# Up group 1 of the second feed-forward as pairs of seven quarter products, with the weight sums made by accumulating transfers

## The reference

```python
def _sqrelu_mlp(h, w1, w2):
    return jnp.square(jax.nn.relu(h @ w1)) @ w2

    h2 = _modulate(_rmsnorm(x, norm2_g), sh2, sc2)
    x = x + g2 * _sqrelu_mlp(h2, w_ff1, w_ff2)
```

## Time and profile before

| | |
|---|---|
| three runs | 1659.97, 1660.47, 1660.49 us |
| median | 1660.47 us |
| profiled execution | 1660.74 us, of which the profile's span is 1659.0 us |
| TensorE busy in the span | 98% |
| VectorE, ScalarE, GpSimd busy | 67%, 46%, 9% |
| second feed-forward | from 1300.7 us of the span to its end |

### The profile page before, as it was taken

The page is one execution under the profiler, slowest core; times in us unless marked ns, Lnnn a source line. Parts: engine busy times, 40 slices in busy tenths (PEclk is TensorE's granted clock), DMA queues, the critical chain, the costliest instruction groups (busy, mean ns, idle before and its releaser), DMA issues. The chain is left out here.

```text
span 1659.0 us, 31156 instructions
## 1 busy us (share of the span) xinstructions
PE 1627.6 (98%) x13194; PEld 1301.0 (78%) x13194; DVE 1110.5 (67%) x1579; ACT 763.0 (46%) x1179; POOL 150.0 (9%) x155
## 2 busy tenths in 40 slices
PE   8999999999999999999999999999999999999997
PEld 6666777777767888888888788886578888998987
DVE  6857689888757477676665772364986656775734
ACT  5444555545255443132323553337776544453523
POOL 0000000000000200001111000031100000414101
PEclk9999999999999999999999999999999999999999
DMA  6212231112145343546563232320102233232321
GB/s 227 87 52 71 79 126 42 41 41 92 42 166 190 119 157 135 175 142 237 189 218 108 78 107 77 110 94 18 28 2 79 87 105 101 87 116 79 125 91 51
DMA packets 51323, 172.89 MB, mean 104 GB/s; under 512 B 6128, under 2 KB 9328, under 8 KB 50416
## 3 DMA queue, kind: packets, MB, share of 16 engines
q1 hardware_dynamic: 41456, 134.71, 24.0%
q0 software_dynamic: 9728, 36.18, 6.5%
HBM read 160.64 MB, written 8.39 MB: 102 GB/s over the span
## 5 line engine op out<-in xcount | busy, mean ns | idle before, releaser
L419 PE MATMUL pair<-h_hi,w_hi 128*128 128x512 f32 (+1 forms) x976 | 379.4, 389 | 4.0 <-DVE h_lo L851 1.5
L466 DVE TENSOR_TENSOR w_lo<-w_raw,w_hi 128x1024 fp32r<-128x1024 f32 (+1 forms) x240 | 280.0, 1172 | 142.9 <-ACT w_hi L444 142.8
L421 PE MATMUL pair<-h_hi,w_lo 128*128 128x512 f32 (+1 forms) x976 | 370.2, 379 | 0.0
L420 PE MATMUL pair<-h_lo,w_hi 128*128 128x512 f32 (+1 forms) x976 | 370.1, 379 | 0.0
L444 ACT CAST w_hi<-w_raw 128x1024 fp32r<-128x1024 f32 (+1 forms) x240 | 224.0, 940 | 219.3 <-PE pair L421 201.9
L419 PEld LDWEIGHTS pair<-h_hi,w_hi 128*128 128x128 f32 x976 | 183.6, 188 | 54.4 <-issue 16.2
L420 PEld LDWEIGHTS pair<-h_lo,w_hi 128*128 128x128 f32 x976 | 183.8, 188 | 35.0 <-issue 2.6
L421 PEld LDWEIGHTS pair<-h_hi,w_lo 128*128 128x128 f32 x976 | 183.6, 188 | 35.1
L419 PE MATMUL pair<-ff_f_hi,w_hi 128*128 128x512 f32 (+1 forms) x536 | 204.2, 381 | 0.6 <-DVE w_lo L466 0.6
L420 PE MATMUL pair<-ff_f_lo,w_hi 128*128 128x512 f32 (+1 forms) x536 | 203.5, 380 | 0.0
L421 PE MATMUL pair<-ff_f_hi,w_lo 128*128 128x512 f32 (+1 forms) x536 | 203.5, 380 | 0.0
(11 more groups left out here) (506 smaller groups left out, 2821.1 us busy)
## 6 DMA issues: line engine op xcount, KB each, us to landing
w_raw<-in_w_ff SPq DMA_DIRECT2D x128, 512.0 KB, 3.5
mod_w<-in_w_mod POOLq DMA_DIRECT2D x48, 512.0 KB, 3.7
w_raw<-in_w_in SPq DMA_DIRECT2D x22, 512.0 KB, 3.4
w_raw<-in_w_gate SPq DMA_DIRECT2D x16, 512.0 KB, 3.5
w_raw<-in_w_out SPq DMA_DIRECT2D x16, 512.0 KB, 3.5
w_raw<-in_w_rwkv SPq DMA_DIRECT2D x15, 512.0 KB, 3.4
w_raw<-in_w_da SPq DMA_DIRECT2D x12, 512.0 KB, 4.8
w_raw<-in_w_ple_gate SPq DMA_DIRECT2D x8, 512.0 KB, 3.5
```

The source lines that it names most:

```text
L419: nc.tensor.matmul(out, w_hi, x_hi, start=(k == 0), stop=False)
L420: nc.tensor.matmul(out, w_hi, x_lo, start=False, stop=False)
L421: last = nc.tensor.matmul(out, w_lo, x_hi, start=False, stop=(k == kt - 1))
L466: nc.vector.tensor_tensor(lo[:, slot, cols], source, hi[:, slot, cols].bitcast(F32), ALU.subtract).then_inc(pr.lo_made, 1)
```

## The change

Up group 1 becomes pairs too, so 12 pairs in place of 8 (`PairedUps(..., 1, ...)`). Three things make room for that:

- The differences are made in jobs 6 and 7 of the stage and split in jobs 8, 9 and 10, all in up group 0. Two of the four change sign or are made by one multiply-and-subtract; the signs are taken back with a scale of -1 in the relu of one half (`positives`).
- GpSimd no longer adds. It issues transfers from HBM that add onto the raw tile in SBUF: `a21` of the second tile becomes `s1` (+ `a22`), then `s2` (+ `a11`), then `s4` (+ `a12`), and `a11` of the first tile becomes `s3` (+ `a21`). Each addition is issued after the split of what stood there: four transfers of 256 KB a pair, and the one that makes `s1` of the next pair is issued behind the one that makes `s4`.
- The units stand in another order, with two units between `s1` and `s2` and between `s2` and `s4`. The fifth product `y` gets a bank half of its own that alternates between bank 6 and bank 2. ScalarE's copy is now of the second unit's bank, and the fifth unit (`w1`) waits for it.

```diff
-    UNITS = (("a11", "b11", "y0"), ("s2", "t2", "x1"), ("a12", "b21", "x0"), ("s3", "t3", "w0"), ("s1", "t1", "y1"), ("s4", "b22", "z0"), ("a22", "t4", "z1"))
-    FIRST, JOIN, NEXT, SPREAD, LAST = 0, 2, 3, 4, 6
+    UNITS = (("s1", "t1", "y"), ("a11", "b11", "w0"), ("a12", "b21", "x0"), ("s2", "t2", "x1"), ("s3", "t3", "w1"), ("a22", "t4", "z1"), ("s4", "b22", "z0"))
+    COPY, JOIN, SPREAD, LAST = 1, 3, 4, 6
+    SPARE = 2
...
     def before(self, pe, Q, i):
         bank = self.UNITS[i][2]
-        if bank == "y1":
+        if bank == "w1":
             pe.wait_ge(self.copied, Q + 1)
-        elif Q and bank in ("w0", "x1", "y0", "z0"):
-            pe.wait_ge(self.joined, 4 * (Q - 1) + {"w0": 2, "x1": 1, "y0": 3, "z0": 4}[bank])
+        elif bank == "y":
+            if Q % 4 == 1:
+                pe.wait_ge(*((self.ff.added, KT * (self.group(Q) - 1)) if self.group(Q) > 1 else (self.ff.relu_made, KT)))
+            if Q > 1:
+                pe.wait_ge(self.joined, 4 * (Q - 2) + 3)
+        elif bank in ("w0", "x0", "z1") and Q:
+            pe.wait_ge(self.joined, 4 * (Q - 1) + {"w0": 2, "x0": 1, "z1": 4}[bank])
...
     def act(self, act, Q, i, bank, done):
-        if i == self.FIRST:
+        if i == self.COPY:
             if Q:
                 act.wait_ge(self.joined, 4 * (Q - 1) + 1)
             act.wait_ge(self.pr.job_done, done)
             self.pr.nc.scalar.copy(self.copy, bank).then_inc(self.copied, 1)
-        if i == 1 and Q % 4:
+        if i == 2 and Q % 4:
             self.positives(act, Q - 1)
...
-        nc.gpsimd.tensor_tensor(s1, a21, a22, ALU.add).then_inc(self.summed, 1)
-        pool.wait_ge(self.summed, 4 * Q + 1)
-        split("s2")
-        nc.gpsimd.tensor_tensor(s2, s1, a11, ALU.subtract).then_inc(self.summed, 1)
-        nc.gpsimd.tensor_tensor(a21, a11, a21, ALU.subtract).then_inc(self.summed, 1)
-        pool.wait_ge(self.summed, 4 * Q + 2)
-        split("s4")
-        nc.gpsimd.tensor_tensor(s4, a12, s2, ALU.subtract).then_inc(self.summed, 1)
+    def add(self, pool, Q, n, name):
+        w = self.pairs[Q] + 1
+        pool.dma_start(self.pr.raw[:, w % RAW_SLOTS, 0:512], self.quarter(Q, name), accum_op=ALU.add).then_inc(self.chain[Q % 2], 16)
+
+    def begin(self, pool, Q):
+        pool.wait_ge(*self.pr.landed(self.pairs[Q] + 1))
+        self.add(pool, Q, 1, "a22")
+
+    def add_third(self, pool, Q):
+        pool.dma_start(self.pr.raw[:, self.pairs[Q] % RAW_SLOTS, 0:512], self.quarter(Q, "a21"), accum_op=ALU.add)\
+            .then_inc(self.third[Q % 2], 16)
 
     def pool(self, pool):
         for Q in range(len(self.pairs)):
-            self.weights(pool, Q)
+            if Q % 4 == 0:
+                self.begin(pool, Q)
+            self.split(pool, Q, "s1")
+            self.add(pool, Q, 2, "a11")
+            self.split(pool, Q, "a11")
+            self.add_third(pool, Q)
+            self.split(pool, Q, "s2")
+            self.add(pool, Q, 3, "a12")
+            if Q % 4 < 3:
+                self.begin(pool, Q + 1)
...
-    TURNED = 2
+    DIFFERENCES = {6: (0, 1), 7: (2, 3)}
+    TURNED = {8: (0, 1), 9: (2,), 10: (3,)}
...
-        self.paired = PairedUps(pr, name, 2, (x_hi, x_lo), self.turned_hi, self.turned_lo, sums, copy,
+        self.paired = PairedUps(pr, name, 1, (x_hi, x_lo), self.turned_hi, self.turned_lo, copy,
```

More of the change, by code:

```diff
@@ L2872, in __init__, with bank @@
         self.pairs = []
-        self.summed, self.copied, self.joined, self.positive, self.squared = (
-            pr.sem(f"{name}_{k}") for k in ("w_sum", "copied", "joined", "positive", "squared"))
-    def bank(self, name):
+        self.chain, self.third = ([pr.sem(f"{name}_{k}{i}") for i in range(2)] for k in ("w_chain", "w_third"))
+        self.copied, self.joined, self.positive, self.squared = (pr.sem(f"{name}_{k}") for k in ("copied", "joined", "positive", "squared"))
+    def bank(self, name, Q):
+        if name == "y":
+            return self.pr.bank[self.SPARE if Q % 2 else 6][:, 0:TC]
         col = TC * int(name[1])
-        return self.pr.bank[4 + "wxyz".index(name[0])][:, col:col + TC]
+        return self.pr.bank[{"w": 4, "x": 5, "z": 7}[name[0]]][:, col:col + TC]
     def job(self, w, Q, i):
@@ L2885, in job @@
         first, second = pr.raw[:, w % RAW_SLOTS, :], pr.raw[:, (w + 1) % RAW_SLOTS, :]
-        raw = {"a11": (first[:, 0:512], pr.landed(w)), "a12": (first[:, 512:1024], pr.landed(w)), "a22": (second[:, 512:1024], pr.landed(w + 1)),
-               "s1": (self.sums[0], (self.summed, 4 * Q + 1)), "s2": (self.sums[1], (self.summed, 4 * Q + 2)),
-               "s3": (second[:, 0:512], (self.summed, 4 * Q + 3)), "s4": (self.sums[2], (self.summed, 4 * Q + 4))}
+        added = lambda n: (self.chain[Q % 2], 16 * (3 * (Q // 2) + n))
+        a11, a21 = first[:, 0:512], second[:, 0:512]
+        raw = {"a11": (a11, pr.landed(w)), "a12": (first[:, 512:1024], pr.landed(w)), "a22": (second[:, 512:1024], pr.landed(w + 1)),
+               "s1": (a21, added(1)), "s2": (a21, added(2)), "s4": (a21, added(3)), "s3": (a11, (self.third[Q % 2], 16 * (Q // 2 + 1)))}
         pr.units[w, i] = raw[source]
-        return Job(w, self.moving[moving], TC, unit=i, bank=self.bank(bank))
+        return Job(w, self.moving[moving], TC, unit=i, bank=self.bank(bank, Q))
     def number(self, g, q):
@@ L2920, in act @@
             self.pr.nc.scalar.copy(self.copy, bank).then_inc(self.copied, 1)
[L2921 removed]
+        if i == 2 and Q % 4:
             self.positives(act, Q - 1)
[L2923 to L2924 removed]
+        if i in (4, 5) and Q % 4:
+            self.high(act, Q - 1, i - 4)
     def positives(self, act, Q):
@@ L2944, in dve @@
         nc, ff = self.pr.nc, self.ff
-        if i in (4, 5) and Q % 4:
-            self.low(dve, Q - 1, i - 4)
+        if i in (5, 6) and Q % 4:
+            self.low(dve, Q - 1, i - 5)
         dve.wait_ge(self.pr.job_done, done)
@@ L3044, in before @@
         kind, g, j, i = self.order[n]
+        if self.paired and kind == "down" and self.paired.first <= g + 1 < FF_GROUPS and j == 3:
+            pe.wait_ge(self.paired.joined, 4 * self.paired.number(g + 1, 3) + 3)
         if kind == "pair":
@@ L3457, in __init__ @@
                                                      for k in range(KT)], width)
-    def turned_at(self, n):
-        kind, g, j, _ = self.order[n]
-        return j if (kind, g) == ("down", self.paired.first - 2) and j < self.TURNED + 4 else None
     def difference(self, dve, t):
-        nc, y, d, h = self.pr.nc, self.y, self.differences, KT // 2
+        nc, y, d = self.pr.nc, self.y, self.differences
         early, late = slice(0, TC), slice(TC, T)
-        one, other = ((y[0][:, :, late], y[0][:, :, early]), (y[1][:, :, late], d[0][:, :, :]), (y[1][:, :, late], y[0][:, :, late]),
-                      (y[1][:, :, early], d[1][:, :, :]))[t]
         if t in (1, 3):
@@ L3538, in act @@
                 .then_inc(self.y_hi, 1)
-        at = self.turned_at(n)
-        if at is not None and at >= self.TURNED:
-            self.turned_act(act, at - self.TURNED)
+        for t in self.TURNED.get(n, ()):
+            self.turned_act(act, t)
         if n in self.SQUARED:
@@ L3569, in dve @@
                 self.low(dve, self.LOW[n], 0, self.LOW[n])
-            at = self.turned_at(n)
-            if at is not None and at >= self.TURNED:
-                self.turned_dve(dve, at - self.TURNED)
+            for t in self.TURNED.get(n, ()):
+                self.turned_dve(dve, t)
             super().dve(dve, n, bank, done)
-            if at is not None and at < self.TURNED:
-                for t in (2 * at, 2 * at + 1):
-                    self.difference(dve, t)
+            for t in self.DIFFERENCES.get(n, ()):
+                self.difference(dve, t)
             return
```

64 lines of the change are left out of this document (34 added, 30 removed).

## The result

Four runs of the changed kernel took 1699.22 to 1701.15 us, median 1700.39; four of the kernel before, beside them, 1660.48. The ratio is 1.024 (95% interval 1.0222 to 1.0258): slower by 39.9 us, outside the range that was given.

What follows compares the result with a forecast made beforehand. TensorE, busy for 98% of the span, was taken as the bound. Group 1 8.11 us later plus 0.44 for groups 2 and 3 made 8.55 us slower: 1669.3 us for the profiled execution, 1669.0 forecast, range 1661 to 1690.

Steps and rivals of the forecast that it cites:

- Group 0: Up group 0, jobs 6 to 10: VectorE's added 10.6 us make group 1's fifth unit start 7.59 us late.
- the rival with short transfers: Paired groups: additions land fast, L = 2.52, the chain is free; 2.2 us slower, 1662.7 us; chance 19%.
- The gains: Group 1 falls from 43.52 to 40.32 us; groups 2 and 3 lose waits of 1.09 us each; at most 5.38 us.
- 3.48 + 2L: Paired groups: period from copy to copy, L from a low half's end to usable data; free up to L = 3.30 us.
- I take 512 KB from GpSimd's queue, 3.7 us: L = 3.92: Paired groups: a 256 KB addition priced as a plain 512 KB transfer; the period becomes 11.32 us.
- the upper bound of 5.02: Paired groups: largest L, from 512 KB landing in 4.8 us with the fullest queue; 29.4 us slower, 1690 us.
- cast of s1 until +0.52: Paired groups, ScalarE: the cast of the next pair's s1 ends 0.52 us after the copy's end.
- additions that queue behind each other: GpSimd's queue in paired groups: one of two ways to a period of 13.52 us or more; chance 13% with the other.
- the rival of slow transfers: Paired groups: L past 5.02 or queued additions, period 13.52 us or more; 1690 us at 5.02; chance 13%.
- the first unit of group 1 before 1347.5: Start of up group 1: a sign of being wrong; the forecast had this unit at 1348.61, 2.15 us late.
- landings of 3.3 to 4.8 us: Paired groups: a sign of being right, the time in which GpSimd's additions land.
- groups 2 and 3 at 40.3 to 45 us: Later paired groups: a sign of being right, the length of each; the forecast had 0.22 us more for each.

Runs made afterwards that it cites:

- the kernel with both edits: Changed kernel with the addition that begins the next pair issued before the wait for s2's split, and all 48 transfers as plain copies: 1673.27 us.
- the kernel that begins early: Changed kernel with the addition that begins the next pair issued behind the pair's third sum, before the wait for s2's split: 1690.83 us.

## Why the prediction was wrong

**Group 0: right.** Taken 1.36 us earlier for the earlier start of job 6, the predicted and measured starts are:

| | predicted, less 1.36 | measured |
|---|---|---|
| job 9 | 1334.84 | 1334.81 |
| job 10 | 1341.13 | 1340.98 |
| first unit | 1347.25 | 1347.01 |
| third unit | 1352.78 | 1352.35 |
| fifth unit | 1358.45 | 1358.22 |

All that is not the transfers was put at 2.2 us slower (the rival with short transfers); with the additions left out it measured 2.6 (0.8 to 3.8).

**The gains: right.** 28 units in 40.3 us and no waits for the spread, as soon as the transfers are out of the way.

**The form of the chain: right.** With the beginning out of the way the path is the one given, 3.48 + 2L. In the kernel with both edits the copies on that path take 3.99 us in the mean, so L = 4.29; by the prediction's sum it would be 15.6 us slower, and it measured 13.2.

**The size of L: wrong.** The step that failed first is "I take 512 KB from GpSimd's queue, 3.7 us: L = 3.92". On the path of the kernel that begins early an addition took 4.70 us in the mean (six of them, group 2), 0.28 from the low half's end to its issue and 0.02 to use it: L = 5.00. That is the upper bound of 5.02, for which the prediction had 1690 us; this kernel took 1690.8, its group 1 ends 14.7 us later (counted from job 6) and groups 2 and 3 take 7.8 and 6.5 us longer, where the price at 5.02 had 15.8 and twice 6.8. So the size of L makes some 22 of the 31 us by which the forecast fell short. The row that the bound came from the earlier trace rows was the nearer one, and the prediction's own remark that the error was upward was not followed. (The Trainium skill, Collectives: The Full Stack, Part 3, gives the two reads as the reason, and half a copy's rate: here a copy of the same 256 KB to the same place lands in 3.1 us and the addition in 4.1, so the whole landing is a third longer and not twice. That the second read is the cause was not tried.)

**The beginning of the next pair: left out.** The second step that failed is "cast of s1 until +0.52" right behind the copy: it takes s1 of the next pair as there. It comes from the transfer issued behind the one for s4, which lands 5.0 to 8.0 us after its issue, so the cast of s1, not the copy, ends the turn, and ScalarE's and VectorE's in-order work behind that cast brings the waits for the spread. This was worth 9.6 us, 1690.8 to 1700.4. It stood in the text as half a rival ("additions that queue behind each other") with 13%; the order of the issues, which stood in the change itself, was enough to see it.

So the rival of slow transfers is what came, with its price (1690 us and more) and with too small a chance. Of the prediction's signs of being wrong one appeared, the first unit of group 1 before 1347.5 (1347.01), but only because job 6 started 1.36 us earlier; the true miss shows at two of its signs of being right, landings of 3.3 to 4.8 us (5.0 to 8.0 where a pair begins) and groups 2 and 3 at 40.3 to 45 us (51.07 and 53.48).

## What to carry to other kernels

When elementwise work is turned into transfers, the question is not how many bytes move but how many landings stand in a row between two uses: here two, with two casts and low halves between them, in 10.08 us of TensorE's time. Price a transfer that others wait for by the slow ones among its neighbours, not by their median, and look at what is issued just ahead of it on its own queue. A lower TensorE clock behind waits was a symptom here where the chain of transfers was the bound, and cost time (1.4 us) only where TensorE was.

## What was not expected of the hardware

- An accumulating transfer of 256 KB keeps GpSimd for 0.859 us, a copy 0.537; it lands in 4.1 us (median) against 3.1.
- Issued 0.5 us behind another, an addition landed in 5.0 to 8.0 us; the one ahead of it in 4.0 to 4.2. Of two copies the second took 3.1 to 5.0, the first 2.8 to 3.7.
- A VectorE instruction on 128 x 1024 elements took 2.2 to 2.3 us beside a GpSimd sum and 1.22 alone; GpSimd's sums took 1.74 to 2.26 us there and 1.3 where VectorE left them alone.
